# The norm squares of a transformer kernel: added on GpSimd and TensorE in place of VectorE

## The chip, the cores and the metric

The kernel runs on one core of a Trainium2 chip. The metric is the device time of one execution in microseconds (us): 2780.21 in the median of three runs.

## The reference, cut to what matters

The whole is one long network over a sequence of 512 tokens with 1024 features, all in fp32: a block with pooling and attention, a feed-forward part, a block with an mLSTM mixer, another feed-forward part, then a second network with a feed-forward part, a mixer, a cross-attention to a memory, and a last feed-forward part. What the change touches is the normalisation that stands ahead of each of these parts and at the end, nine times in all:

```python
def rms_norm(x):
    y = x * lax.rsqrt(jnp.mean(x * x, axis=-1, keepdims=True) + EPS)
    return y          # then times a scale (or gain), plus a shift
```

The mean is over the 1024 features of each token.

## The kernel before, in words

**Layout.** `x` lies transposed: features on the 128 partitions, in `KC` = 8 chunks of 128 features, tokens along the free dimension (512). Weights arrive in units of 128x2048 by DMA into two `raw` slots. ScalarE copies a unit to a rounded high part (`split_hi`, line 195), VectorE subtracts it to get the low part (`split_lo`, line 199), and TensorE does three matmuls for each product (lines 212 to 214).

**Order.** Each stage has a method for each engine, and each engine's program is the list of its methods, stage after stage; nothing is scheduled beside that. Engines meet through semaphores that count up. An engine works strictly in its own order, so what it waits for holds up everything behind.

**A norm** (class `Norm`) does this. ScalarE squares each chunk as soon as it is ready (`square`, line 408, into `sq[:, k, :]`, eight chunks of 128x512; ahead of chunk 4 it loads an activation table, line 406). VectorE adds chunks 1 to 7 one after the other into chunk 0 (`add_square`, line 415: seven adds of 128x512 in a norm, 63 in all). TensorE sums over the partitions with `sum_features` (line 448): four matmuls, one for each 128 tokens, with a column of ones as the moving side; the profile records each fp32 matmul as two instructions, so a norm has eight. ScalarE takes the root (line 420), VectorE the inverse (line 425), TensorE spreads it to a row (`spread_row`, line 456), VectorE scales each chunk (line 431), ScalarE rounds it to `h_hi` (line 436) and VectorE takes the rest `h_lo` (line 441), which the next stage's matmuls read.

**Where the nine norms stand.** They are numbered 0 to 8.

- Norm 0 is at the start. VectorE's share lies in `Conditioning.vector`: products of eight weight units with the condition (line 310), adds between them, then two splits, then the last add in `Norm.vector`. TensorE sums the conditioning's 16 blocks first (`sum_rows`, line 337).
- Norms 2, 4, 5 and 8 follow a feed-forward stage (`FeedForward`). Its last unit runs block by block: six matmuls finish one of eight banks, VectorE updates that chunk of `x` (line 628) and adds an earlier square; before these updates it has one weight split to do, except at the very end. Norm 8 is the final one.
- Norms 1, 3, 6 and 7 follow a `Project` stage, four weight units of two chunks each; its last unit updates chunks 6 and 7 at once (line 530). In norm 1 TensorE also does the sums of the conditioning around `sum_features` (`with_ada`). Norm 6 belongs to the stage `Memory`, where `sum_features` and `spread_row` stand between weight units on TensorE.

**GpSimd** issues three DMAs at the start, pads and pools in the stage `Even` (lines 991 to 1009), and later issues two more DMAs (lines 2139 and 2141), each behind a wait. SyncE issues all other DMAs.

Of the kernel before, what the change touches and what calls it, by code (L numbers as in the profile page):

```python
# [19 lines left out]
ALU = mybir.AluOpType  # L20
# [6 lines left out]
P = 128  # L27
D = 1024
S = 512
KC = D // P  # L30
TB = S // P
# [70 lines left out]
def program(nc, xT, memT, stream, params, tables, even_tables, mix_tables, w_pool, outT):  # L102
    ctx = ExitStack()
    with ctx:
# [27 lines left out]
        def area(start, *shape):  # L132
            n = int(np.prod(shape))
            assert start + n <= WORK, (start, shape)
            v = work[:, start:start + n]
            if len(shape) == 2:
                v = v.rearrange("p (a b) -> p a b", a=shape[0])
            if len(shape) == 3:
                v = v.rearrange("p (a b c) -> p a b c", a=shape[0], b=shape[1])
            return v  # L140
# [5 lines left out]
        bank = ctx.enter_context(nc.psum_tensor("bank", [P, 8, 512], F32))  # L146
# [8 lines left out]
        ident, ones = table("ident"), table("ones")  # L155
# [24 lines left out]
        def slot(m):  # L180
            return m % 2
# [87 lines left out]
        class Conditioning:  # L269
# [50 lines left out]
            def vector(self, dve, st):  # L320
                dve.wait_ge(setup_loaded, 32)
                dve.wait_ge(self.silu_done, 1)
                for n in range(ADA_FIRST):
                    self.add_unit(dve, n)
                    if n >= 2:
                        self.norm.add_square(dve, n - 1)
                split_lo(dve, 0)
                split_lo(dve, 1)
                self.write_mod(dve, st, 0, 1)
                dve.sem_inc(self.mod_done, 1)  # L330
# [35 lines left out]
        sq_done = sem("sq_done")  # L366
        sq_added = sem("sq_added")
        ms_done = sem("ms_done")
# [7 lines left out]
        class Norm:  # L376

            ROW = 6  # L380
            root, inv = small[:, 480:480 + TB], small[:, 484:484 + TB]

            def __init__(self, scale, shift, free_bank, before=None, final=False, late=True):
# [23 lines left out]
                self.wait_x(act, k)  # L407
                nc.scalar.activation(self.sq[:, k, :], x[:, k, :], ACT.Square).then_inc(sq_done, 1)

            def add_square(self, dve, k):  # L410

                dve.wait_ge(sq_done, KC * self.n + k + 1)
                if k > 1:
                    dve.wait_ge(sq_added, (KC - 1) * self.n + k - 1)
                nc.vector.tensor_tensor(self.sq[:, 0, :], self.sq[:, 0, :], self.sq[:, k, :],
                                        ALU.add).then_inc(sq_added, 1)

            def take_root(self, act):
                act.wait_ge(ms_done, self.n + 1)
# [23 lines left out]

            def sum_features(self, pe):

                pe.wait_ge(sq_added, (KC - 1) * (self.n + 1))
                for t in range(TB):
                    last = nc.tensor.matmul(bank[:, self.bank, t:t + 1], self.sq[:, 0, t * P:t * P + P],
                                            ones[:, 0:1], start=True, stop=True)
                last.then_inc(ms_done, 1)  # L450

            def spread_row(self, pe):

# [16 lines left out]
                        split_next_hi(act, self.late)  # L470

            def vector(self, dve, st):
                self.add_square(dve, KC - 1)
                self.take_inverse(dve)
                for k in range(KC):
                    self.scale_chunk(dve, k)
                    if k and not self.final:
                        self.low(dve, k - 1)
                if not self.final:
                    self.low(dve, KC - 1)  # L480
                    if self.late is not None:
                        split_next_lo(dve, self.late)
                    if self.with_ada:
                        conditioning.write_mod(dve, st, 3, 6)
# [13 lines left out]
        class Project:  # L498
# [20 lines left out]
            def vector(self, dve, st):  # L519
                for u in range(4):  # L520
                    m = self.m0 + u
                    if self.during:
                        self.during.prepare_vector(dve, st, u)
                    if u:
                        for k in range(max(1, 2 * u - 2), 2 * u):
                            self.after.add_square(dve, k)
                    dve.wait_ge(unit_used, m + 1)
                    for b in range(2):
                        o = 2 * u + b
                        nc.vector.scalar_tensor_tensor(x[:, o, :], bank[:, 2 * slot(m) + b, :], self.gate(o),  # L530
                                                       x[:, o, :], ALU.mult, ALU.add).then_inc(x_ready, 1)
                    if u < 3:
                        split_next_lo(dve, m)
                self.after.add_square(dve, KC - 2)
                if self.after.late is None:
                    self.after.add_square(dve, KC - 1)
                    split_next_lo(dve, self.last_unit)

            def tensor(self, pe):
# [22 lines left out]
        class FeedForward:  # L562
# [41 lines left out]
            def vector(self, dve, st):  # L604
                def block(r, i):
                    m, b = self.m0 + r, 2 * slot(self.m0 + r)
                    dve.wait_ge(silu_done, self.j0 + r + 1 + 2 * i)
                    nc.vector.tensor_tensor(self.gu[:, r, :], self.silu[:, r, :], bank[:, b + 1, :],  # L608
                                            ALU.mult).then_inc(gated, 1)
                    dve.wait_ge(g_hi_done, self.j0 + r + 1 + 2 * i)  # L610
                    nc.vector.tensor_tensor(g_lo[:, bass.ds(2 * i + r, 1), :], self.gu[:, r:r + 1, :],  # L611
                                            g_hi[:, bass.ds(2 * i + r, 1), :], ALU.subtract).then_inc(g_ready, 1)
                    split_next_lo(dve, m, i)

                with dve.Fori(0, FB // 2) as i:
                    block(0, i)
                    block(1, i)
                split_next_lo(dve, self.md)
                with dve.Fori(0, 4) as i:
                    split_next_lo(dve, self.md + 1, i)  # L620
                    split_next_lo(dve, self.md + 2, i)
                split_next_lo(dve, self.md + 9)
                for o in range(KC):
                    if o < KC - 1:
                        dve.wait_ge(down_block, (KC - 1) * self.f + o + 1)
                    else:
                        dve.wait_ge(unit_used, self.md + 11)
                    nc.vector.scalar_tensor_tensor(x[:, o, :], bank[:, o, :], self.gate(o), x[:, o, :],
                                                   ALU.mult, ALU.add).then_inc(x_ready, 1)
                    if o >= 2:  # L630
                        self.after.add_square(dve, o - 1)

            def tensor(self, pe):
                def block(r, i, first=False):
# [266 lines left out]
        class Even:  # L901
            PAD = 8
            W = S + 2 * PAD
            u = area(0, 4, W)
# [8 lines left out]
            inv, t = area(19968, S), area(20480, 2, S)  # L913
# [214 lines left out]
        class Mlstm:  # L1128
# [10 lines left out]
            o = area(12352, TB, D)  # L1139
# [291 lines left out]
        class Hgrn:  # L1431
# [6 lines left out]
            q, k, b = area(0, H, S), area(2048, H, S), area(4096, H, S)  # L1438
# [469 lines left out]
        class Memory:  # L1908
            HEADS = 4
            mt, sq, t = area(8192, KC, N_MEM), area(10240, KC, N_MEM), area(12288, KC, N_MEM)  # L1910
# [130 lines left out]
        def gain_of(name):  # L2041
            return lambda k: col(name, k)

        def constant(name):
            return lambda k: col(name)

        DOWN, OUT = 0, 4
        conditioning = Conditioning()
        stages = [conditioning]

        def add(stage):
            stages.append(stage)
            return stage
# [3 lines left out]
        even = add(Even(norm))  # L2057
        last = add(Project("even_out", shift_of(0, 2), even.wait_chunk))
        norm = add(Norm(scale_of(0, 4), shift_of(0, 3), OUT, last))
        norm.with_ada = True  # L2060
        last = add(FeedForward("ffn0", shift_of(0, 5), norm))
        norm = add(Norm(scale_of(1, 1), shift_of(1, 0), DOWN, last))
        odd = add(Mlstm(norm))
        last = add(Project("odd_out", shift_of(1, 2), odd.wait_chunk))
        norm = add(Norm(scale_of(1, 4), shift_of(1, 3), OUT, last))
        last = add(FeedForward("ffn1", shift_of(1, 5), norm))
        norm = add(Norm(gain_of("ffn1_norm"), constant("zero"), DOWN, last))
        last = add(FeedForward("ffn2", constant("half"), norm))
        mix_tables_free = KC * updates[0]
        norm = add(Norm(gain_of("mix_norm"), constant("zero"), DOWN, last))  # L2070
        mix = add(Mix(norm))
        memory = Memory()
# [4 lines left out]
        norm = add(Norm(gain_of("ffn2_norm"), constant("zero"), OUT, last))  # L2077
        last = add(FeedForward("ffn3", constant("half"), norm))
        final = add(Norm(gain_of("final_norm"), constant("zero"), DOWN, last, final=True))
        n_units = N_UNITS  # L2080

        block = ctx.enter_context(nc.Block())
# [49 lines left out]
        @block.gpsimd  # L2132
        def _(pool):
            pool.dma_start(area(16384, 4 * S), even_tables[:, 0:4 * S]).then_inc(even_loaded, 16)
            pool.dma_start(area(18432, 2 * S), even_tables[:, 4 * S:6 * S]).then_inc(even_loaded, 16)
            pool.dma_start(area(19456, 4 * P), w_pool[:, :]).then_inc(even_loaded, 16)
            even.gpsimd(pool)
            pool.wait_ge(x_ready, mix_tables_free)
            pool.dma_start(area(24064, MIX_TABLES), mix_tables[:, :]).then_inc(mix_loaded, 16)
            pool.wait_ge(mix.hg.s_summed, mix.hg.H)  # L2140
            pool.dma_start(area(8192, KC * N_MEM), memT[:, :]).then_inc(mem_loaded, 16)

        @block.scalar
        def _(act):
# [140 lines left out]
```

## Time and profile before

| | |
|---|---|
| median of three runs | 2780.21 us (2776.09 to 2782.19) |
| the profiled execution | span 2781.3 us; no separate time of it is shown |
| TensorE busy | 2622.8 us, 94%, 12226 matmul instructions |
| TensorE weight loads | 2134.9 us, 77% |
| VectorE busy | 1193.5 us, 43% |
| ScalarE busy | 923.1 us, 33% |
| GpSimd busy | 27.9 us, 1%, 29 instructions |
| mean granted TensorE clock | 0.937 of full speed |

How to read it: the span runs from the first to the last instruction of one execution. Busy shares are means over stages with different limits; since TensorE is busy most of the time, what counts is where it stands still, and what it waits for there. The granted clock is a share of 2.4 GHz; 0.50 is 1.2 GHz.

### The profile page before, as it was taken

To read this page: it belongs to the slowest core of one execution; us is meant where nothing else is said; L and a number is where in the kernel's file an instruction comes from. 1 tells how busy PE (TensorE), PEld (TensorE's weight loads), DVE (VectorE), ACT (ScalarE), POOL (GpSimd) and SP (SyncE) were. 2 spreads that over 40 slices of the span, in tenths; PEclk is the share of its full clock that TensorE was granted. 3 is DMA by queue.
4 is the path that set the end of the run, shared out by engine and by line. 5 is a ranking of instruction groups with operands and counts; after the bars stand their busy time and mean duration, and the time that the engine had idled before them with its cause. 6 is when DMAs were issued, how large, how long until landed. Compare 5 with 4: busy or idle time off the path is not lost.

```text
span 2781.3 us, 30671 instructions
## 1 busy us (share of the span) xinstructions
PE 2622.8 (94%) x12226; PEld 2134.9 (77%) x12226; DVE 1193.5 (43%) x1511; ACT 923.1 (33%) x1297; POOL 27.9 (1%) x29
## 2 busy tenths in 40 slices
PE   3899999999989979999999999999988999999998
PEld 2656788888869657888887888879866887788886
DVE  5266543332273465333224333145666543533323
ACT  2212333331233443333124332134444434333312
POOL 0300000000000000000000000000000000000000
PEclk9955589999999989999999999999989999999999
DMA  6346412222213101222222222222210140222221
GB/s 253 145 159 222 154 61 93 104 90 105 91 61 107 46 1 61 92 104 90 105 92 76 93 103 91 97 96 76 73 49 1 70 143 31 76 106 90 94 103 61
DMA packets 36883, 261.75 MB, mean 94 GB/s; under 512 B 4096, under 2 KB 4224, under 8 KB 5696
## 3 DMA queue, kind: packets, MB, share of 16 engines
q1 hardware_dynamic: 36144, 256.90, 25.7%
q0 software_dynamic: 656, 3.67, 0.4%
q8 instruction: 61, 1.00, 0.2%
q14 instruction: 22, 0.18, 0.0%
HBM read 258.46 MB, written 2.10 MB: 94 GB/s over the span
## 4 chain that ended last, share of the span: by engine, by line
PE 87%; DVE 7%; ACT 3%; DMA 2%; issue 1%; SPq 0%; DVEq 0%; ACTq 0%
PE bank L212 22%; PE bank L214 22%; PE bank L213 22%; PE bank L835 3%; PE bank L853 2%; PE bank L243 2%; PE bank L244 2%; PE bank L249 2%; PE bank L1426 2%; PE bank L844 1%; DMA raw<-stream 1%; DVE w_lo L199 1%; ACT w_hi L195 1%; PE bank L337 1%; PE bank L1706 1%
## 5 line engine op out<-in xcount | busy, mean ns | idle before, releaser
L199 DVE TENSOR_TENSOR w_lo<-raw,w_hi 128x2048 fp32r<-128x2048 f32 x192 | 440.4, 2294 | 654.3 <-ACT w_hi L195 654.3
L212 PE MATMUL bank<-h_hi,w_hi 128*128 128x512 f32 x1824 | 714.4, 392 | 5.0 <-DVE h_lo L441 3.8
L214 PE MATMUL bank<-h_hi,w_lo 128*128 128x512 f32 x1824 | 711.7, 390 | 0.0
L213 PE MATMUL bank<-h_lo,w_hi 128*128 128x512 f32 x1824 | 711.4, 390 | 0.0
L195 ACT ACTIVATE w_hi<-raw 128x2048 fp32r<-128x2048 f32 x192 | 366.1, 1907 | 448.3 <-PE bank L214 416.1
L212 PEld LDWEIGHTS bank<-h_hi,w_hi 128*128 128x128 f32 x1824 | 343.0, 188 | 79.3 <-DVE h_lo L441 4.3
L214 PEld LDWEIGHTS bank<-h_hi,w_lo 128*128 128x128 f32 x1824 | 343.0, 188 | 71.8
L213 PEld LDWEIGHTS bank<-h_lo,w_hi 128*128 128x128 f32 x1824 | 343.3, 188 | 70.2
L213 PE MATMUL bank<-g_lo,w_hi 128*128 (+1 forms) x704 | 279.4, 397 | 0.0
L214 PE MATMUL bank<-g_hi,w_lo 128*128 (+1 forms) x704 | 279.4, 397 | 0.0
L212 PE MATMUL bank<-g_hi,w_hi 128*128 (+1 forms) x704 | 279.4, 397 | 0.0
L608 DVE TENSOR_TENSOR work<-work,bank 128x512 f32<-128x512 f32 x88 | 60.6, 688 | 459.9 <-ACT work L582 459.9
L582 ACT ACTIVATE work<-bank 128x512 f32<-128x512 f32 x88 | 52.7, 599 | 554.7 <-PE bank L214 535.1
L213 PEld LDWEIGHTS bank<-g_lo,w_hi 128*128 128x128 f32 x704 | 132.8, 189 | 32.1
L214 PEld LDWEIGHTS bank<-g_hi,w_lo 128*128 128x128 f32 x704 | 132.8, 189 | 32.1
L212 PEld LDWEIGHTS bank<-g_hi,w_hi 128*128 128x128 f32 x704 | 132.8, 189 | 32.1
L212 PE MATMUL bank<-w_hi,h_hi 128*128 128x256 f32 (+1 forms) x480 | 137.2, 286 | 0.9 <-DVE w_lo L199 0.9
L213 PE MATMUL bank<-w_lo,h_hi 128*128 128x256 f32 (+1 forms) x480 | 135.8, 283 | 0.0
L214 PE MATMUL bank<-w_hi,h_lo 128*128 128x256 f32 (+1 forms) x480 | 135.8, 283 | 0.0
L611 DVE TENSOR_TENSOR g_lo<-work,g_hi 128x512 f32 x88 | 61.0, 693 | 81.2 <-ACT g_hi L584 81.2
L212 PEld LDWEIGHTS bank<-w_hi,h_hi 128*128 128x128 f32 x480 | 92.3, 192 | 1.1 <-DVE w_lo L199 1.0
L213 PEld LDWEIGHTS bank<-w_lo,h_hi 128*128 128x128 f32 x480 | 92.3, 192 | 0.1
(237 smaller groups left out, 2809.2 us busy)
## 6 DMA issues: line engine op xcount, KB each, us to landing
raw<-stream SPq DMA_DIRECT2D x200, 1024.0 KB, 4.9
ring<-stream SPq DMA_DIRECT2D x40, 1024.0 KB, 4.9
x<-xT SPq DMA_DIRECT2D x1, 2048.0 KB, 17.8
outT<-work SPq DMA_DIRECT2D x8, 256.0 KB, 2.2
work<-even_tables POOLq DMA_DIRECT2D x1, 1024.0 KB, 9.5
work<-memT POOLq DMA_DIRECT2D x1, 1024.0 KB, 5.2
tab<-tables SPq DMA_DIRECT2D x1, 888.0 KB, 5.6
work<-mix_tables POOLq DMA_DIRECT2D x1, 768.0 KB, 4.5
```

The costliest lines, as they stand in the source:

```text
L195: nc.scalar.activation(w_hi[:, slot(m), :], raw[:, slot(m), :], ACT.Copy).then_inc(hi_split, 1)
L199: nc.vector.tensor_tensor(w_lo[:, slot(m), :], raw[:, slot(m), :], w_hi[:, slot(m), :], ALU.subtract).then_inc(lo_split, 1)
L212: nc.tensor.matmul(out, stationary[0], moving[0], start=first, stop=False)
L213: nc.tensor.matmul(out, stationary[0], moving[1], start=False, stop=False)
L214: return nc.tensor.matmul(out, stationary[1], moving[0], start=False, stop=last)
L243: nc.tensor.matmul(out[:, b, :], wh[:, k, r], h_hi[:, k, :], start=(k == 0), stop=False)
L244: nc.tensor.matmul(out[:, b, :], wl[:, k, r], h_hi[:, k, :], start=False, stop=False)
L249: last = nc.tensor.matmul(out[:, b, :], wh[:, k, r], h_lo[:, k, :], start=False, stop=(k == KC - 1))
L608: nc.vector.tensor_tensor(self.gu[:, r, :], self.silu[:, r, :], bank[:, b + 1, :], ALU.mult).then_inc(gated, 1)
L611: nc.vector.tensor_tensor(g_lo[:, bass.ds(2 * i + r, 1), :], self.gu[:, r:r + 1, :], g_hi[:, bass.ds(2 * i + r, 1), :], ALU.subtract).then ...
L835: last = nc.tensor.matmul(bank[:, 4 + s % 2, 0:self.keys], q, k, start=(a == 0), stop=(a == len(pairs) - 1))
L853: last = nc.tensor.matmul(bank[:, t % 2, 0:self.n_out], self.pt[:, t % 2, k * P:k * P + P], self.values(t, k), start=(k == 0), stop=(k == ...
```

## The change

VectorE no longer adds squares. GpSimd adds chunks 1 to 5 into chunk 0, in a new method `Norm.gpsimd`. TensorE sums three chunks over the partitions, chunk 0 (with 1 to 5 in it), 6 and 7, into the same four columns of a bank; only the very first matmul has `start` set. GpSimd's program runs through the norms in order around what it did before.

```diff
             def vector(self, dve, st):            # Conditioning
                 for n in range(ADA_FIRST):
                     self.add_unit(dve, n)
-                    if n >= 2:
-                        self.norm.add_square(dve, n - 1)
...
-            ROW = 6
+            ROW, ADDS = 6, KC - 3
...
-            def add_square(self, dve, k):
-
-                dve.wait_ge(sq_done, KC * self.n + k + 1)
-                if k > 1:
-                    dve.wait_ge(sq_added, (KC - 1) * self.n + k - 1)
-                nc.vector.tensor_tensor(self.sq[:, 0, :], self.sq[:, 0, :], self.sq[:, k, :],
-                                        ALU.add).then_inc(sq_added, 1)
+            def gpsimd(self, pool):
+
+                for k in range(1, self.ADDS + 1):
+                    pool.wait_ge(sq_done, KC * self.n + k + 1)
+                    if k > 1:
+                        pool.wait_ge(sq_added, self.ADDS * self.n + k - 1)
+                    nc.gpsimd.tensor_tensor(self.sq[:, 0, :], self.sq[:, 0, :], self.sq[:, k, :],
+                                            ALU.add).then_inc(sq_added, 1)
...
             def sum_features(self, pe):
 
-                pe.wait_ge(sq_added, (KC - 1) * (self.n + 1))
-                for t in range(TB):
-                    last = nc.tensor.matmul(bank[:, self.bank, t:t + 1], self.sq[:, 0, t * P:t * P + P],
-                                            ones[:, 0:1], start=True, stop=True)
-                last.then_inc(ms_done, 1)
+
+                def add_chunk(k):
+                    for t in range(TB):
+                        last = nc.tensor.matmul(bank[:, self.bank, t:t + 1], self.sq[:, k, t * P:t * P + P],
+                                                ones[:, 0:1], start=(k == 0 and t == 0), stop=(k == KC - 1),
+                                                skip_group_check=True)
+                    return last
+
+                pe.wait_ge(sq_added, self.ADDS * (self.n + 1))
+                add_chunk(0)
+                pe.wait_ge(sq_done, KC * self.n + KC - 1)
+                add_chunk(KC - 2)
+                pe.wait_ge(sq_done, KC * self.n + KC)
+                add_chunk(KC - 1).then_inc(ms_done, 1)
...
             def vector(self, dve, st):            # Norm
-                self.add_square(dve, KC - 1)
                 self.take_inverse(dve)
...
             def vector(self, dve, st):            # Project
-                    if u:
-                        for k in range(max(1, 2 * u - 2), 2 * u):
-                            self.after.add_square(dve, k)
...
-                self.after.add_square(dve, KC - 2)
                 if self.after.late is None:
-                    self.after.add_square(dve, KC - 1)
                     split_next_lo(dve, self.last_unit)
...
                     nc.vector.scalar_tensor_tensor(x[:, o, :], bank[:, o, :], self.gate(o), x[:, o, :],
                                                    ALU.mult, ALU.add).then_inc(x_ready, 1)   # FeedForward
-                    if o >= 2:
-                        self.after.add_square(dve, o - 1)
...
+        norms_to_mix = [stage for stage in stages[2:stages.index(mix)] if isinstance(stage, Norm)]
+        norms_after_mix = [memory.norm] + [stage for stage in stages[stages.index(mix):] if isinstance(stage, Norm)]
...
-            even.gpsimd(pool)
+            for stage in (conditioning.norm, even, *norms_to_mix):
+                stage.gpsimd(pool)
             pool.wait_ge(x_ready, mix_tables_free)
             pool.dma_start(area(24064, MIX_TABLES), mix_tables[:, :]).then_inc(mix_loaded, 16)
             pool.wait_ge(mix.hg.s_summed, mix.hg.H)
             pool.dma_start(area(8192, KC * N_MEM), memT[:, :]).then_inc(mem_loaded, 16)
+            for stage in norms_after_mix:
+                stage.gpsimd(pool)
```

## Rows read from the trace of the kernel before

**Rows 1.** The page: busy time of GpSimd and others, and the chain that ended last

```profile
PE 2622.8 (94%) x12226; PEld 2134.9 (77%) x12226; DVE 1193.5 (43%) x1511; ACT 923.1 (33%) x1297; POOL 27.9 (1%) x29
...
PE 87%; DVE 7%; ACT 3%; DMA 2%; issue 1%; SPq 0%; DVEq 0%; ACTq 0%
```

**Rows 2.** Timeline, norm 4: start us, us, engine, line, operation, count, [idle before <-releaser]

```profile
1453.88 2.06 DVE L628 SCALAR_TENSOR_TENSOR x<-bank,mod,x 128x512 f32<-128x512 f32 x3
...
1461.85 0.75 DVE L628 SCALAR_TENSOR_TENSOR x<-bank,mod,x 128x512 f32<-128x512 f32 x1
1462.52 1.48 DVE L415 TENSOR_TENSOR work<-work 128x512 f32<-128x512 f32 x2
...
1454.66 1.95 ACT L408 ACTIVATE work<-x 128x512 f32<-128x512 f32 x3 [3.02 <-DVE x L628]
...
1458.03 1.28 ACT L406 ACT_TABLE_LOAD   x1
1459.32 1.21 ACT L408 ACTIVATE work<-x 128x512 f32<-128x512 f32 x2
...
1464.05 1.05 PE L448 MATMUL bank<-tab,work 128*128 128x1 f32 x8 [3.20 <-DVE work L415]
```

**Rows 3.** Timeline, norm 3, after a projection: squares 6 and 7, then the sums

```profile
1087.08 1.29 ACT L408 ACTIVATE work<-x 128x512 f32<-128x512 f32 x2 [7.21 <-DVE x L530]
...
1089.28 1.05 PE L448 MATMUL bank<-tab,work 128*128 128x1 f32 x8 [3.03 <-DVE work L415]
```

**Rows 4.** Timeline of TensorE, norm 1: conditioning sums, then the norm's

```profile
378.35 4.86 PE L337 MATMUL bank<-tab,work 128*128 128x1 f32 x32
383.06 1.85 PE L448 MATMUL bank<-tab,work 128*128 128x1 f32 x8
```

**Rows 5.** Timeline of TensorE, norm 6: the sums between two weight units

```profile
2215.95 0.95 PE L448 MATMUL bank<-tab,work 128*128 128x1 f32 x8
2216.76 0.37 PE L212 MATMUL bank<-mem_hi,w_hi 128*128 128x256 f32 x1
```

**Rows 6.** Timeline of TensorE, norm 0: conditioning sums, then the norm's

```profile
42.88 6.96 PE L337 MATMUL bank<-tab,work 128*128 128x1 f32 x32 [42.88 <-DVE work L310]
53.19 1.86 PE L448 MATMUL bank<-tab,work 128*128 128x1 f32 x8 [3.35 <-DVE work L415]
```

**Rows 7.** GpSimd's tensor operations: timeline, by line (ns min/median/max), by form

```profile
83.22 1.09 ACT L1025 ACTIVATE work<-bank 128x512 f32<-128x512 f32 x2 [7.99 <-PE bank L214]
...
84.49 1.06 POOL L1002 TENSOR_TENSOR work<-work 128x527 f32<-128x527 f32 x1 [11.94 <-ACT work L1025]
85.63 1.09 POOL L1008 TENSOR_TENSOR work<-work 128x512 f32<-128x512 f32 x1
86.80 3.22 POOL L1009 TENSOR_TENSOR work<-work 128x512 f32<-128x512 f32 x1
...
86.15 2.72 DVE L199 TENSOR_TENSOR w_lo<-raw,w_hi 128x2048 fp32r<-128x2048 f32 x1 [8.59 <-ACT w_hi L195]
...
L199 DVE TENSOR_TENSOR w_lo<-raw,w_hi x192: 2275/2293/2718, 46.8 to 2747.8; 128x2048 fp32r<-128x2048 f32 x192
...
L1009 POOL TENSOR_TENSOR work<-work x4: 1285/1291/3217, 86.8 to 109.2; 128x512 f32<-128x512 f32 x4
...
L1002 POOL TENSOR_TENSOR work<-work 128x513 f32<-128x513 f32 x1 | 1.3, 1298 | 0.1
```

**Rows 8.** Timeline, norm 8, the final one: squares 5 and 6, then the sums

```profile
2766.25 0.63 ACT L408 ACTIVATE work<-x 128x512 f32<-128x512 f32 x1 [0.24 <-DVE x L628]
2767.65 0.63 ACT L408 ACTIVATE work<-x 128x512 f32<-128x512 f32 x1 [0.77 <-DVE x L628]
...
2770.47 1.05 PE L448 MATMUL bank<-tab,work 128*128 128x1 f32 x8 [2.24 <-DVE work L415]
```

**Rows 9.** Stretches, norms 2 and 5: us, busy PE, PEld, DVE, ACT, POOL, clock, DMA

```profile
768.60:769.80 1.20, 1.05 (x8) 0.97 (x8) 0.01 (x1) 0.04 (x1) 0.00 (x0) 0.92 0.00 0
...
1837.40:1838.90 1.50, 1.41 (x8) 1.33 (x8) 0.00 (x0) 0.00 (x0) 0.00 (x0) 0.69 0.76 143
```

## The prediction

> **What bounds the kernel now.** I read the page first: TensorE is busy 94% of the span and carries 87% of the chain that ended last, GpSimd 1% [rows 1]. So a microsecond counts only where TensorE waits, or where it is given more to do. The change touches the nine norms, 0 to 8 in order of the stages. I therefore went through the timeline around each of the nine column sums and read three things: how long TensorE stood still before them, what released them, and whether TensorE was working without a gap.
>
> Three kinds of norm come out. After a feed-forward stage (norms 2, 4, 5 and 8) and after the projections of norms 3 and 7, TensorE idles some 3 us before the sums, and the last add on VectorE releases it [rows 2, 3]. In norm 1 TensorE works without a gap through the sums [rows 4], and so it does in norm 6, where they lie between two weight units [rows 5]. In norm 0 they wait for an add queued behind the first splits [rows 6].
>
> **The parts.** (a) 63 adds leave VectorE, two of them 1.48 us in one run [rows 2]. (b) 45 adds go to GpSimd, five a norm, each waiting for its square and for the add before it. (c) TensorE sums three chunks (the added one, 6, 7) in place of one: 8 more matmuls a norm, recorded as 16 instructions. (d) The DMAs of the mix tables and of the memory keep their places behind waits that come later than the adds in front of them, so I price them at nothing. The group opens its bank once and nothing else is written there meanwhile; it adds no wait.
>
> **Price of four column sums.** In an unbroken stream at full clock, 0.81 us from their start to the next matmul [rows 5]; the last group of a chain counts 1.05 until its result is out [rows 2]. At the half clock 32 instructions take 6.96 us, 0.2175 each [rows 6], so a group is 1.74. Three groups at full clock are 2 x 0.81 + 1.05 = 2.67 us.
>
> **Price of an add on GpSimd.** The trace has no such add of norm squares. Nearest are its tensor operations on 128x512. One takes 1.09 us [rows 7], line 1009 has 1.29 as its median, and line 1002, an add, took 1.06 at its first call and 1.30 in its shortest form, 128x513 [rows 7]. That form adds a row to itself eight elements on; by the code the quick ones are those with an odd or small offset between their inputs, and the squares lie 512 elements apart or more. So I take 1.29, and keep 1.09 as the low end. Between dependent ones lie 0.08 us (84.49 + 1.06 to 85.63), and 0.18 passed from the end of the releasing ScalarE instruction (84.31) to the first [rows 7]. I take 0.1 from GpSimd to TensorE.
>
> **Norms 2, 4, 5.** Take norm 4, in us after its first x update (1453.88) [rows 2]. The last block's matmul ends at 6.97 (sums start at 1464.05 after 3.20 idle), each block takes 1.40 (two squares of the last norm are that far apart [rows 8]). Before, update 7 started at 7.97, one us behind its block, because update and add share VectorE; squares, add 6, add 7 followed, and the sums ran from 10.17 to 11.22. After, VectorE does only updates: update 7 starts at 7.0, square 7 ends at 8.4. Alone that would be a gain. But the first chunk waits for GpSimd. Squares 0 to 2 end at 2.73, so square 1 at about 2.05; squares 4 and 5 are held by the table load, and end at about 5.3 and 5.9 when all before comes 0.7 earlier. GpSimd: add 1 from 2.23, then one every 1.37, add 4 from 6.34, add 5 from 7.71 to 9.0. TensorE starts at 9.1 and ends at 11.77, against 11.22: **+0.55**. In norms 2 and 5 the clock matters. In their windows it was granted at 0.92 and 0.69 on average, so it fell from 2.4 to 1.2 GHz after 1.0 us of the first and 0.6 us of the second [rows 9], at 11.1 and 10.7 on this scale, after about 4 us without a dense matmul. Norm 2 does some 20 of the 24 instructions by then and four at half clock, end 12.1, **+0.9**; norm 5 16 and eight, end 12.6 against 11.58 (its sums took 1.41 [rows 9]), **+1.0**. Together +2.45.
>
> **Norm 8.** No split lies ahead, so VectorE was not late there. Square 5 ends at 2766.88 [rows 8]; add 4 runs from about 2766.2, add 5 ends at 2768.85, sums 2768.95 to 2771.62 against 2771.52 [rows 8]: **+0.1**.
>
> **Norms 3 and 7.** The five adds are done a unit earlier, under the matmuls of the last unit; were that cover gone, the case of norm 4 would apply. In norm 3 the last matmul ends at 1086.25, the two squares run from 1087.08 to 1088.37, the sums ended at 1090.33 [rows 3]. After: chunk 0 at once, chunk 6 from 1087.75, chunk 7 (its square is ready by then) until 1087.75 + 0.81 + 1.05 = 1089.6. **-0.7 each, -1.4.**
>
> **Norm 1.** The sums stand between 32 instructions of conditioning sums and 16 more, and the stretch is already at half clock (8 instructions in 1.85 us) [rows 4]. Sixteen more are 16 x 0.2175 = **+3.5**, with nothing to cover them.
>
> **Norm 6.** Same, at full clock: 2 x 0.81 = **+1.6** [rows 5].
>
> **Norm 0.** Before, the sums waited 3.35 us behind 32 others and ended at 55.05 [rows 6]. After, 24 instructions follow the 32 directly: 49.84 + 5.2 = 55.05, no change. The adds taken out of the weight products could let one of the two load chains run 0.6 us earlier; adds on GpSimd beside these products could cost 0.4 (2.72 against a median of 2.29 for a split beside GpSimd work [rows 7]). I take **-0.2**.
>
> Next late in every norm is what was late before: root, inverse, row, scaling. Their order stays.
>
> Sum: -0.2 + 3.5 + 2.45 - 1.4 + 1.6 + 0.1 = **+6.05 us**. The profiled execution has a span of 2781.3, 1.1 us above the median of 2780.2 and within the runs shown (2776.1 to 2782.2), so I add the sum to the median: 2786.2.
>
> **A rule weighed.** GpSimd's subtraction at 86.80 took 3.22 us in place of 1.29 beside a split (86.15, itself 2.72), and ended 1.15 after it [rows 7]: it was held while a VectorE instruction with two inputs from SBUF ran. The trace has no GpSimd work beside an x update, which reads one input from PSUM. The Trainium skill (SBUF — State Buffer, Who interferes with whom) says that a VectorE instruction with at most one SBUF input, outside the two-port modes, does not contend with GpSimd, and one with two does if GpSimd reads SBUF. The row agrees with the second half; by the first half, the next case but one does not happen.
>
> **Rivals.** *GpSimd is quick (0.27), not slower than before.* Place: the five adds after a feed-forward stage; price 1.09 each. For it: line 1008's row [rows 7]; against: the 1.29 of the others. Add 5 ends at 8.0, TensorE 8.1 to 10.75: -0.5 in norms 2 and 4, -0.8 in 5, -0.4 in 8, so the sum is -0.2 + 3.5 - 1.8 - 1.4 + 1.6 - 0.4 = +1.3, 2781.5. It decides below about 1.18 us an add, where the sums of norm 4 end no later than before. By the Trainium skill (GPSIMD Engine Reference, Elementwise — side-by-side cycle accounting) an fp32 add of 2048 elements takes 4497 ns; a quarter, 1.12 us, is an estimate, and by it the time would be about 2782; the 1.29 of the row speaks against it.
>
> *GpSimd is held by the x updates too (0.13), slower still.* Each update is 0.75 us and each block has one [rows 2]. Five adds then meet some 3.5 us of updates, add 5 ends at 12.5, past the fall of the clock, and the three groups take 5.3: the end is near 17.9, +6.5 in each of norms 2, 4 and 5 against +0.8 above, and +1.5 in norm 8. Sum about +25, 2805. For it: the one held instruction [rows 7]; against: an update has one SBUF input, and the held ones stood beside splits.
>
> **How the numbers follow.** My forecast has 0.55, the two rivals 0.27 and 0.13, and 0.05 stays for what I don't see. A measurement tells about 0.2%, 5.6 us, from no change, and the forecast lies on that border: about two thirds of it fall above. Slower: 0.36 + 0.13 + 0.02 = 0.51; the same: 0.19 + 0.22 + 0.01 = 0.42; faster: 0.05 of the first rival and 0.02 = 0.07. The forecast's own range is 2783 to 2790. The range reaches down over the first rival to 2780 and up to 2795 for a partial hold or an earlier fall of the clock.
>
> **What would show it.** Adds on GpSimd near 1.29 us in the timeline; in norm 4 the sums start about 2.1 us after the last dense matmul in place of 3.2, released by GpSimd, and end later than before; 24 instructions without a gap in norm 1 and in norm 6; in norms 3 and 7 the root 0.7 us earlier after the last dense matmul. I am wrong if the sums of norms 2, 4 and 5 are released by ScalarE, if they start after 10, or if norm 1 is not longer by 3 us.

## The result and the profile after

The changed kernel takes 2791.72 us (four executions, 2789.87 to 2793.75) against 2780.49 of the kernel before: a ratio of 1.0042, 95% interval 1.003 to 1.0053. It is slower by 11.2 us, where 6 were forecast. Run again later it came to 1.0034 (1.0016 to 1.0052).

The span of the profiled execution is 2788.0 us, 6.7 above that of before. The difference of the two traces is smaller than that of the medians because the profiled execution of before was a slow one of its kind (its whole time was 2783.2) and that of after the quickest of its four (2789.9). I therefore compare the traces norm by norm, not as wholes.

The page of the kernel after, next to [rows 1]:

```profile
span 2788.0 us, 30923 instructions
PE 2639.3 (95%) x12370; PEld 2152.7 (77%) x12370; DVE 1156.5 (41%) x1448; ACT 923.2 (33%) x1297; POOL 102.8 (4%) x74
```

VectorE has lost 63 instructions and 37 us of busy time; the execution is longer all the same. TensorE has 144 more and is busy 16.5 us longer. Now the timeline of norm 4, kernel after, to be laid beside [rows 2]:

```profile
1453.50 3.55 DVE L630 SCALAR_TENSOR_TENSOR x<-bank,mod,x 128x512 f32<-128x512 f32 x5
...
1460.50 0.75 DVE L630 SCALAR_TENSOR_TENSOR x<-bank,mod,x 128x512 f32<-128x512 f32 x1 [0.65 <-PE bank L214]
...
1461.29 0.63 ACT L406 ACTIVATE work<-x 128x512 f32<-128x512 f32 x1 [0.77 <-DVE x L630]
...
1455.64 7.01 POOL L414 TENSOR_TENSOR work<-work 128x512 f32<-128x512 f32 x5 [371.74 <-ACT work L406]
...
1462.71 4.01 PE L448 MATMUL bank<-tab,work 128*128 128x1 f32 x24 [2.25 <-POOL work L414]
...
1467.28 2.08 PE L464 MATMUL bank<-tab,small 128*128 128x128 f32 x8 [0.56 <-DVE small L424]
```

Update 7 starts 7.00 us after the first one, not 7.97: VectorE is no longer late. But the sums are released by GpSimd, at 9.21 on that scale, while square 7 had ended at 8.42. And the three groups take 4.01 us, not 2.67. The granted clock in the same stretch (columns as in [rows 9]):

```profile
1460.50:1462.70 2.20, 0.00 (x0) 0.00 (x0) 0.75 (x1) 0.65 (x2) 2.02 (x2) 1.00 0.00 0
1462.70:1464.70 2.00, 1.99 (x16) 1.99 (x16) 0.00 (x0) 0.00 (x0) 0.00 (x0) 0.86 0.00 0
1464.70:1466.70 2.00, 2.00 (x10) 1.93 (x10) 0.00 (x0) 0.00 (x0) 0.00 (x0) 0.50 0.00 0
```

The clock is at 2.4 GHz as long as TensorE idles, and falls to 1.2 GHz while it does the one-column matmuls, 3.7 us after the last dense one. The same view of norm 6, where nothing stands still:

```profile
2219.70:2222.70 3.00, 3.00 (x26) 3.00 (x26) 0.76 (x1) 0.00 (x0) 0.00 (x0) 0.87 0.29 63
2222.70:2225.00 2.30, 2.30 (x11) 2.30 (x12) 0.18 (x1) 2.06 (x3) 0.00 (x0) 0.50 0.91 381
2225.00:2228.00 3.00, 3.00 (x16) 3.00 (x15) 2.29 (x1) 0.49 (x1) 0.00 (x0) 0.50 0.00 0
```

TensorE is busy without a gap, and the clock falls all the same, some 2 us into the 24 one-column instructions, and stays down for some 6 us of the weight unit behind them. So the spread row started 8.7 us later than before by the trace's own time, of which 3.8 had been there ahead of the sums. Norms 3, 7, 1 and 0 of the kernel after, beside [rows 3, 4, 6]:

```profile
1087.70 0.95 PE L448 MATMUL bank<-tab,work 128*128 128x1 f32 x8
1089.37 1.95 PE L448 MATMUL bank<-tab,work 128*128 128x1 f32 x16 [0.72 <-ACT work L406]
...
2401.62 2.53 PE L448 MATMUL bank<-tab,work 128*128 128x1 f32 x16 [0.72 <-ACT work L406]
...
377.14 3.63 PE L335 MATMUL bank<-tab,work 128*128 128x1 f32 x32
380.63 3.92 PE L448 MATMUL bank<-tab,work 128*128 128x1 f32 x24
...
50.53 5.26 PE L448 MATMUL bank<-tab,work 128*128 128x1 f32 x24
```

**The measure used from here on.** For each norm, the time from the end of the last 256- or 512-column matmul ahead of the sums to the start of the first one behind them (norm 0: from the start of the span; norm 8: to the root), less the same in the trace before, where they are 59.45, 21.62, 9.43, 8.48, 8.44, 9.00, 0.65, 8.48 and 3.33 us. A negative number is a stretch that became shorter. Worked out from the timelines, one trace of each kernel:

```
norm                       0     1     2     3     4     5     6     7     8    sum
forecast                -0.2  +3.5  +0.9  -0.7 +0.55  +1.0  +1.6  -0.7  +0.1   +6.1
changed                 +0.7  +0.8  +2.3  -0.8  +2.2  +1.7  +2.2   0.0  +0.2   +9.3
changed, again          +1.0  +2.6  +0.8  -0.6  +2.4  +2.0  +1.8  -0.6  +0.2   +9.6
VectorE adds, 3 groups  +0.1  +0.4  -0.3  -0.8   0.0  -0.8  +2.1  -0.5  -0.4   -0.2
GpSimd adds all seven   -1.7  -1.0  +3.0  +1.9  +2.9  +2.3  +0.1  +2.0  +1.6  +11.1
chunk 0 last            +0.7  +0.5  -0.8  -0.8  -0.6  -2.1  +1.8  -0.6  +0.2   -1.7
mixed                   -0.4  -0.1  +1.5  -0.2  +1.5  +1.0   0.0  -0.7  +0.2   +2.9
mixed, chunk 0 last     -0.4  -0.4  -1.3  -0.5  -1.3  -1.4   0.0  -0.5  +0.2   -5.6
norm 6 alone             0.0  -0.3   0.0   0.0   0.0   0.0  +1.8  +0.4   0.0   +1.8
128 columns             -1.1  -2.8   0.0  -1.4  +0.2  +1.3  +1.8  -1.4  +0.3   -3.1
before, 128 columns     -0.1  -2.8  +0.6  +0.9  +0.5  -0.3   0.0  +1.0  +0.1    0.0
mixed, last, 128        +0.1  -2.9  -1.6  -1.4  -1.4  -2.0   0.0  -1.4  +0.3  -10.4
chunk 0 last, 128       +0.3  -2.9  -1.6  -1.4  -1.4  -2.0  +1.8  -1.4  +0.3   -8.4
```

### The profile page after: what moved, and what is told of

Same layout as the page of the kernel before. It is cut to its first block, busy times and chain, and to the rows that moved or that the text cites. A ratio compares the mean times of both kernels' runs of the same rounds, so it can differ in the third digit from the quotient of the medians.

```text
span 2788.0 us, 30923 instructions
## 1 busy us (share of the span) xinstructions
PE 2639.3 (95%) x12370; PEld 2152.7 (77%) x12370; DVE 1156.5 (41%) x1448; ACT 923.2 (33%) x1297; POOL 102.8 (4%) x74
## 4 chain that ended last, share of the span: by engine, by line
PE 87%; DVE 6%; ACT 3%; DMA 1%; issue 1%; POOL 1%; SPq 0%; POOLq 0%; DVEq 0%; ACTq 0%
PE bank L212 22%; PE bank L214 22%; PE bank L213 22%; PE bank L835 2%; PE bank L853 2%; PE bank L243 2%; PE bank L1426 2%; PE bank L244 2%; PE bank L249 2%; PE bank L335 1%; PE bank L844 1%; DVE w_lo L199 1%; PE bank L448 1%; DMA raw<-stream 1%; ACT w_hi L195 1%
## 5 line engine op out<-in xcount | busy, mean ns | idle before, releaser
L414 POOL TENSOR_TENSOR work<-work 128x512 f32<-128x512 f32 x45 | 74.9, 1664 | 2404.4 <-ACT work L406 2400.5
```

What stands on the lines that cost most here:

```text
L414: nc.gpsimd.tensor_tensor(self.sq[:, 0, :], self.sq[:, 0, :], self.sq[:, k, :], ALU.add).then_inc(sq_added, 1)
```

## The experiments

**Theory A**: the loss comes where GpSimd's chain of adds ends late, after the feed-forward stages. **Theory B**: it is TensorE's own extra column sums. Later, **C**: the one-column matmuls let the clock fall; **D**: the gap ahead of them does. Each ratio is to executions of the kernel before that ran beside the variant (29 each time, medians 2780.03, 2780.15 and 2780.3 us). All kernels below put the seven calls of `add_square` back into VectorE's program; tables say for each norm which engine adds, how many squares, and in what order TensorE takes the chunks, and the matmul has a width:

```diff
+                self.eng, self.adds, self.order = ADDER[self.n], ADDS[self.n], ORDER[self.n]
+                self.added = sum(ADDS[:self.n])
...
+                chunks = [0] + list(range(self.adds + 1, KC))
+                if self.order == "zero_last":
+                    chunks = chunks[1:] + [0]
...
+                        last = nc.tensor.matmul(bank[:, self.bank, t * WIDE:t * WIDE + WIDE],
+                                                self.sq[:, k, t * P:t * P + P], ones[:, 0:WIDE],
```

### The adds back on VectorE

```diff
-ADDER = ['pool'] * 9      # the changed kernel
+ADDER = ['dve'] * 9
 ADDS = [5] * 9
```

> The changed kernel with the adds of chunks 1 to 5 back on VectorE at their former places; TensorE still sums chunks 0, 6 and 7. Theory A (the loss is GpSimd's late add chain after the feed-forward stages): in norms 2, 4 and 5 the sums start about 8 us after the first x update in place of 9.2, and end near 10.6, before the 11.2 of the kernel before; some 8 us less than the changed kernel, about 2783. Theory B (the loss is TensorE's own extra column sums, wherever they stand): they are all still there, so the time stays within 2 us of the changed kernel's 2791.

Measured: 2779.84 us, ratio 1.0005 (0.9993 to 1.0018) to the kernel before. The loss is gone with all of TensorE's extra sums still there, which speaks for theory A and against B. Norm 4 of this kernel:

```profile
1445.51 2.95 PE L475 MATMUL bank<-tab,work 128*128 128x1 f32 x24 [1.14 <-DVE work L423]
```

The sums start 8.11 us after the first update (1437.40) and 1.1 after the last dense matmul, in place of 2.25, and end inside the time at full clock but for the last few. Theory A had named 2783; it came out 3 lower.

### All adds on GpSimd

```diff
-ADDS = [5] * 9
+ADDS = [7] * 9            # TensorE sums one chunk
```

> All seven adds on GpSimd, TensorE sums one chunk as before. Theory A: the seventh add ends about 12.0 us after the first x update in norms 2, 4 and 5, the sums end at 13 to 14 against 11.2 before; +2.3 in each, +1.3 in norm 8, +1.4 in each of norms 3 and 7, nothing in 0, 1 and 6, where TensorE is busy: about +11, 2791. Theory B: TensorE has no more work than before, so the time is that of the kernel before within 3 us.

Measured: 2794.36 us, 1.0059 (1.0046 to 1.0073), +14 where theory A had +11 and theory B none. Norm 4 of this kernel, its adds and its sums:

```profile
1456.87 9.81 POOL L434 TENSOR_TENSOR work<-work 128x512 f32<-128x512 f32 x7 [366.71 <-ACT work L416]
...
1466.73 1.87 PE L475 MATMUL bank<-tab,work 128*128 128x1 f32 x8 [5.04 <-POOL work L434]
```

A late add costs at full price, and with the same small sums as before the clock is down by the time they come (1.87 us for 8 instructions against 1.05). Norms 0 and 1 came out 1.7 and 1.0 us shorter, where the expectation had nothing; no run takes that apart.

### Chunk 0 last

```diff
-ORDER = ['zero_first'] * 9
+ORDER = ['zero_first'] * 2 + ['zero_last', 'zero_first', 'zero_last', 'zero_last', 'zero_first', 'zero_first', 'zero_last']
```

> The changed kernel, but in norms 2, 4, 5 and 8 TensorE takes chunks 6 and 7 first and chunk 0, the one that waits for GpSimd, last. Theory A: two of three groups run under GpSimd's chain, so the sums end near 10.3 to 10.7 us after the first x update in place of 13; 2.3 less in three norms and 1 less in norm 8, about 8 less than the changed kernel, 2783. Theory B: the same instructions in another order, no more than 2 us less.

Measured: 2780.45 us, 1.0008 (0.9997 to 1.0019), some 10 us less than the changed kernel, with the same instructions. Norm 4:

```profile
1457.94 1.05 PE L475 MATMUL bank<-tab,work 128*128 128x1 f32 x8
1459.34 1.95 PE L475 MATMUL bank<-tab,work 128*128 128x1 f32 x16 [0.35 <-ACT work L416]
```

Chunk 6 is summed at once after the last block, and what TensorE waits for next is the square of chunk 7, for 0.35 us; GpSimd is not seen any more. By the table norms 2, 4 and 5 turn from +2.1 on average to -1.2.

### Mixed

```diff
-ADDER, ADDS = ['pool'] * 9, [5] * 9
+ADDER = ['dve', 'dve', 'pool', 'pool', 'pool', 'pool', 'dve', 'pool', 'pool']
+ADDS = [7, 7, 5, 5, 5, 5, 7, 5, 5]
```

> Norms 0, 1 and 6, in which TensorE had no gap ahead of the sums, are as in the kernel before (seven adds on VectorE, one chunk summed); the other six as changed. Theory A: these three cost some 3.7 us in the two traces (0.7, 0.8 and 2.2), so about 2787 to 2788 and most of the loss stays. Theory B: a third of the extra TensorE work is gone and with it all of it that had no cover; more than 6 us less, 2785 or below.

Measured: 2780.16 us, 1.0002 (0.9991 to 1.0014). By the whole time this is theory B's number, and a miss for A. By the trace norms 0, 1 and 6 are back to before (-0.4, -0.1, 0.0), 4.2 less than changed, as theory A had it. Norms 2, 4 and 5 cost 1.5, 1.5 and 1.0 here, less than in the changed kernel, because the clock fell later: the 24 instructions of norm 4 took 3.33 us in place of 4.01. The trace leaves +2.9, within the interval of the runs at its upper end. So A alone is not the whole; both parts cost, and the clock adds to either.

```profile
1460.14 3.33 PE L475 MATMUL bank<-tab,work 128*128 128x1 f32 x24 [2.23 <-POOL work L434]
```

### Norm 6 alone

```diff
 ADDER = ['dve'] * 9
-ADDS = [7] * 9            # the kernel before
+ADDS = [7, 7, 7, 7, 7, 7, 5, 7, 7]
```

> The kernel before, but in norm 6 alone VectorE adds five squares and TensorE sums three chunks between its two weight units. Extra work without cover: the sums of norm 6 take 2.4 to 3.2 us of the stream in place of 0.8, +1.6 (theory A and B alike), or +2.2 where the clock falls in them, and the stage behind it takes part of that back: 2780 to 2783, hardly to be told from no change. A cost above 4 us would mean that this place carries more of the loss than the traces show.

Measured: 2781.21 us, 1.0007 (0.9994 to 1.0021), and +1.8 in norm 6 by the trace, the clock at full speed throughout this time:

```profile
2215.00:2217.00 2.00, 2.00 (x19) 2.00 (x19) 0.18 (x1) 1.36 (x3) 0.00 (x0) 1.00 0.69 279
2217.00:2219.00 2.00, 2.00 (x20) 2.00 (x19) 0.77 (x1) 1.19 (x1) 0.00 (x0) 1.00 0.46 193
```

That is the price of 16 more instructions without cover and without a fall of the clock. It also shows that one-column sums in this place do not always bring the clock down: of the five traces with 24 of them here it fell in two (the changed kernel and the one with VectorE adds) and held in three (this one, chunk 0 last, and the changed kernel run again).

### 128 columns in place of one

The changed kernel with its order; each column sum is written as 128 equal columns, and the root reads one of them.

```diff
-WIDE = 1
+WIDE = 128
...
-                nc.scalar.activation(self.root, bank[:, self.bank, 0:TB], ACT.Sqrt, bias=eps,
+                nc.scalar.activation(self.root, bank[:, self.bank, 0:TB * WIDE:WIDE], ACT.Sqrt, bias=eps,
```

> The changed kernel, with every column sum of the norms written as a matmul with 128 columns of ones in place of one (the root reads the first column of each block; 128 columns took no longer than one where both are seen: 1.05 us for 8 instructions at full clock, spread row and sums). Theory C (the clock falls during the sums because TensorE does next to nothing in a one-column matmul, and so half of the loss in norms 2, 4, 5 and 6 is clock): the three groups take 2.7 to 3.1 us in place of 4.0 to 4.3, norm 6 keeps 2.4 GHz through the sums and the unit behind it, and the spread rows get faster too; 5 us or more less than the changed kernel, 2786 or below. Theory D (the clock falls because of the gap ahead of the sums, whatever follows): norms 2, 4 and 5 stay at 4.0 us, time unchanged within 2 us of 2791.

Measured: 2772.14 us, 0.9975 (0.9957 to 0.9993), which is 19 less than the changed kernel (17 less than when that was run again) and 8 less than the kernel before. Theory C, and by more than it had named. Norm 4, the same sums 128 columns wide, and its spread row:

```profile
1451.26 2.94 PE L475 MATMUL bank<-tab,work 128*128 128x128 f32 x24 [2.24 <-POOL work L434]
1454.77 1.16 PE L485 MATMUL bank<-tab,small 128*128 128x128 f32 x8 [0.57 <-DVE small L444]
```

The gap ahead is the same as in the changed kernel (2.24 against 2.25), so the gap alone, theory D, is not what let the clock fall. The sums take 2.94 in place of 4.01, and the spread row 1.16 in place of 2.08. In norm 6 they take 2.84 and the unit behind them stays at 2.4 GHz; since it did so in three of five traces with one column too, this norm decides nothing.

What decides is the count over norms 2, 3, 4, 5 and 7 of all traces with three groups: with one column (six traces) the clock fell in all 30 cases, 1.0 to 5.0 us after the sums had begun; with 128 columns (three traces, with those of the last two kernels below) it kept 2.4 GHz for at least 6.4 us in 14 of 15. In norm 1 the clock was down when the 24 wide instructions began, came back during them, and the 16 one-column instructions behind took 1.84 us in place of 3.55. Wide sums are no cure for the gap: in the fifteenth case, norm 5 of this trace, the clock fell 0.2 us after the sums had begun, the 24 instructions took 4.57 us, and only the spread row was quick again (1.16). The norms account for 12.4 of the 19 us (+9.3 to -3.1). The rest lies in stages between the norms, 3.4 us less between norms 2 and 3 for one. Two kernels with one column are as much shorter there (mixed 3.4, norm 6 alone 3.1), so that part is not shown to come from the wide sums; what part of the rest they caused stays open.

### The kernel before with 128 columns

```diff
 ADDER, ADDS = ['dve'] * 9, [7] * 9      # the kernel before
-WIDE = 1
+WIDE = 128
```

> The kernel before (seven adds on VectorE, one chunk summed), only with 128-column sums. Theory C: its sums are short and the gap of 3 us ahead of them is there still; at most norm 5 (1.41 us) and some spread rows gain, -1 to -3. Theory D: no change.

Measured: 2779.64 us, 0.9994 (0.998 to 1.0009): no change. With 3 us of idle time ahead one wide group did not hold the clock: in norms 2, 3, 4 and 7 it fell between 0.2 us before the sums and 0.8 us into them. In norm 4 the group took 1.35 us against 1.05 [rows 2] and the spread row was at half clock:

```profile
1456.35 1.35 PE L475 MATMUL bank<-tab,work 128*128 128x128 f32 x8 [3.20 <-DVE work L423]
1458.27 2.07 PE L485 MATMUL bank<-tab,small 128*128 128x128 f32 x8 [0.57 <-DVE small L444]
```

The zero of the table is made of opposites: norms 2, 3, 4 and 7 are 0.5 to 1.0 us longer than in the trace before, norm 1 is 2.8 shorter. The latter is not the width's: the 32 one-column conditioning sums ahead of it, which are the same in both kernels, ran at 2.4 GHz here and took 3.63 us in place of 4.86 [rows 4], and the clock fell later. So wide sums paid where three groups began at most 2.3 us after the last dense matmul, and one group behind a gap of 3 us gained nothing.

### The parts together

Mixed engines with chunk 0 last in norms 2, 4, 5 and 8:

```diff
 ADDER, ADDS = (as in the mixed kernel)
-ORDER = ['zero_first'] * 9
+ORDER = ['zero_first'] * 2 + ['zero_last', 'zero_first', 'zero_last', 'zero_last', 'zero_first', 'zero_first', 'zero_last']
```

> Norms 0, 1 and 6 as in the kernel before, norms 3 and 7 as changed, norms 2, 4, 5 and 8 as changed but with chunks 6 and 7 summed first. Theory A: from the traces of the two parts norms 2, 4 and 5 are 0.6 to 1.5 shorter each than before, 3 and 7 about 0.6, 8 even; -4 against the kernel before, 2776. Theory B: each of these six norms still has 16 more instructions on TensorE, so no better than before.

Measured: 2773.06 us, 0.9974 (0.9966 to 0.9983). Three better than theory A had named; B falls, since six norms still have their 16 extra instructions.

The same with `WIDE = 128`:

> The same with 128-column sums. Theory C: where the clock fell between the sums and the spread row it now stays up, 0.5 to 1 us more in each of norms 2, 3, 4, 5 and 7 than without: -8 against the kernel before, 2772. Theory D: as without, 2776.

Measured: 2767.84 us, 0.9957 (0.9944 to 0.9971), theory C again. Norms 2, 3, 5 and 7 gain 0.3 to 1.0 over the one without. Norm 1 gains 2.5, but the clock was up here before its one wide group began (3.63 us for the 32 sums ahead), so that is not shown to be the width's.

The changed kernel (GpSimd adds five squares in every norm) with that order and `WIDE = 128`:

> The changed kernel with 128-column sums and, in norms 2, 4, 5 and 8, chunks 6 and 7 summed first. Theories A and C together: by the traces of the two parts, norm by norm, 0: -1.0, 1: -2.8, 2: -1.6, 3: -1.4, 4: -1.4, 5: -2.0, 6: +1.9, 7: -1.4, 8: +0.3, together -9.4 against the kernel before, 2771 or a little less; if one of the two repairs already holds all there is to gain, no better than the 2772 of the wide sums alone by more than 1.

Measured: 2763.0 us, 0.9948 (0.9928 to 0.9967), 17 us better than the kernel before and 27 better than the changed one run beside it. Of its twelve executions five lie at 2753 to 2756, see the end; its slowest, 2772.6, is 11 us below the slowest of the kernel before in that batch, where the norms account for 8.4. It beats both kernels with two edits in `sum_features` and one in `take_root`. Its norm 4, last dense matmul to first, is 7.0 us against 8.4:

```profile
1435.77 1.16 PE L475 MATMUL bank<-tab,work 128*128 128x128 f32 x8
1437.17 2.05 PE L475 MATMUL bank<-tab,work 128*128 128x128 f32 x16 [0.24 <-ACT work L416]
1439.78 1.16 PE L485 MATMUL bank<-tab,small 128*128 128x128 f32 x8 [0.57 <-DVE small L444]
```

### The changed kernel again

No edit.

> The changed kernel as it stands, again, beside the runs that follow. 2790 to 2794 as in its first four executions if they were typical; if the stretch of the first attention stage comes out quick in some executions, as it did in some of the kernel before and of the other variants, single ones 10 us below that.

Measured: 2789.61 us in the median, 1.0034 (1.0016 to 1.0052), from 2773.5 to 2793.5. By norm its trace repeats the first in the sum (+9.6), while norms 1 and 2 have changed roles (+2.6 and +0.8 for +0.8 and +2.3): where the clock falls moves from one execution to the next.

## Why the prediction was right, and where it was off

The sign, the range (2780 to 2795) and the mechanism (sums released by GpSimd after the feed-forward stages, extra sums without cover elsewhere) held; the sum was a little over half of what came, and 2791.7 lies above the forecast's own 2783 to 2790. The part of the range above 2790 had been kept for a partial hold of GpSimd or an earlier fall of the clock, and it was the fall that came. There is luck in the total: norms 2, 4 and 5 cost 3.7 us more than forecast and norm 1 cost 2.7 less, and one hid most of the other. One of the prediction's own signs of being wrong came true, too: norm 1 is not longer by 3 us in either trace. By its own steps:

- **Norms 2, 4 and 5**, forecast +2.45, found +6.2 in the first trace and +5.2 in the second. The chain of adds was right: the forecast start of the sums was 9.1 us after the first update, and 9.21 was found; I took 1.29 us for an add, and 1.30 is the median. The gap between dependent adds was 0.14 and not 0.08 (five in 7.01 us). The mis-sized term is the length of the three groups. I took 2.67 us in norm 4, because there the clock had held before, and let it fall in the others where it had fallen before. It fell 3.4, 3.7 and 3.7 us after the last dense matmul in norms 2, 4 and 5 (from the clock shares of the windows), and the groups took 4.27, 4.01 and 4.03. The time at which it fell in one trace was no property of that norm.
- **Norm 6**, forecast +1.6: the 16 instructions are that (+1.8 alone). The fall of the clock in them, in the first trace, was not foreseen; it took 2.7 us more until the spread row, of which the stage gave 2.3 back, since it waits elsewhere.
- **Norm 1**, forecast +3.5, found +0.8 and +2.6. This is the term that was over-sized. The price was that of a half clock over the whole stretch; in the first trace the 32 instructions ahead ran at 2.4 GHz and took 3.63 us in place of 4.86, and the 24 behind them took 3.92, not the 5.2 of the half clock.
- **Norm 0**, forecast -0.2, found +0.7 and +1.0. The adds beside the weight products cost both sides; the products ran 5.63 and 6.39 us for two where one alone takes 2.35, and the five adds took 12.67:

```profile
21.58 12.67 POOL L414 TENSOR_TENSOR work<-work 128x512 f32<-128x512 f32 x5 [18.56 <-ACT work L406]
...
22.83 5.63 DVE L310 SCALAR_TENSOR_TENSOR work<-raw,cond,work 128x2048 f32<-128x2048 f32 x2 [5.52 <-DMA raw<-stream]
30.00 6.39 DVE L310 SCALAR_TENSOR_TENSOR work<-raw,cond,work 128x2048 f32<-128x2048 f32 x2 [1.54 <-DMA raw<-stream]
```

- **Norms 3 and 7**, forecast -0.7 each: -0.8 and -0.6 where the clock held; 0.0 in norm 7 of the first trace, whose 16 instructions took 2.53 us in place of 1.95. **Norm 8**, +0.1: +0.2, and 0.7 more behind the root, where the spread row took 1.87 in place of 1.16.
- **Between the norms** the first trace was 3.4 us shorter than before, which hid part of the loss in the spans; I had nothing for it.

The first rival (GpSimd quick) fell: no undisturbed add below 1.26 us. The second (GpSimd held by the x updates) fell as well:

```profile
L414 POOL TENSOR_TENSOR work<-work x45: 1261/1298/3313, 21.6 to 2773.3; 128x512 f32<-128x512 f32 x45
```

Its median, 1.298, is that of an add alone, and the updates kept 0.75 us. The longest add, 3.313, is in norm 0 beside a weight product with two inputs in SBUF. The Trainium skill (SBUF — State Buffer, Who interferes with whom) says that a VectorE instruction with at most one SBUF input, outside the two-port modes, does not contend with GpSimd, and that one with two does if GpSimd reads SBUF; these two readings agree with it.

## What to carry to other kernels

Before work is moved to a slower engine, ask which result its consumer takes first: the same adds cost some 10 us or nothing by the order in which TensorE read the chunks, because the chunk that waits for the slow engine stood first in the program of an engine that works in order. And a handful of one-column matmuls is not cheap filler for TensorE: where the next dense work is some microseconds away, they ran into a fall of the clock that the same matmuls with 128 columns, at nearly the same length, avoided in 14 of 15 places, though not behind a gap of 3 us. Price such a stretch at both clocks, and do not read from one trace which of them a place will get.

## What the runs showed of the hardware that I had not expected

- The granted clock fell from 2.4 to 1.2 GHz though TensorE stood still nowhere: in norm 6 of the changed kernel, some 2 us into a row of 24 one-column instructions right behind dense work. It did so in two of five traces; with 128 columns it held there in both traces that have them. At full clock the width costs next to nothing: 24 instructions take 2.94 us in norm 4 against 2.84 with one column in norm 8 of the changed kernel. In the best kernel all sums and spread rows of norms 2 to 8 ran at 2.4 GHz.
- The executions of one kernel scatter over 4 to 21 us. The first attention stage, between norms 0 and 1, takes some 319 us mostly at 1.2 GHz; in the profiled execution of the kernel with VectorE adds it took 14.4 us less, and a part of it ran at the full clock. The same stretch, before and in that kernel:

```profile
200.00:240.00 40.00, 40.00 (x123) 26.27 (x122) 23.63 (x30) 10.38 (x27) 0.00 (x0) 0.50 0.51 184
```

```profile
200.00:240.00 40.00, 35.58 (x164) 22.66 (x164) 33.85 (x42) 13.83 (x36) 0.00 (x0) 0.80 0.72 263
```

  The profiled execution of the best kernel is another of these (0.80 there too, 14.1 us less). What sets it off was not tried. In that batch two of 29 executions of the kernel before lay below 2770 us, and five of 12 of the best one below 2756: whether the wide sums ahead of the stage make it likelier stays open, and so does how much of that kernel's 17 us is this.
